# Product 4's second Strassen step in nine more groups, and the rotation in the next group's first four units

## The reference

```python
h = rmsnorm(x, norm_g[layer])
proj = h @ w_in[layer]                      # 1024 x 1024 @ 1024 x 12288
b_a, c_a, x_a, z_a, q, k, v, z_b, g_a, g_b = jnp.split(proj, split_points, axis=-1)
y_a = short_conv_branch(b_a, c_a, x_a, z_a, conv_w[layer], conv_b[layer], w_a_out[layer])
y_b = retention_branch(q, k, v, z_b, w_b_out[layer])   # q and k turned by rotary()
merged = jax.nn.sigmoid(g_a) * y_a + jax.nn.sigmoid(g_b) * y_b
x = x + merged @ w_o[layer]

def rotary(t, cos, sin):
    t1, t2 = jnp.split(t, 2, axis=-1)
    return jnp.concatenate([t1 * c - t2 * s, t1 * s + t2 * c], axis=-1)
```

## Time and profile before

| what | us |
|---|---|
| median of 3 runs | 1373.87 (1373.47 to 1374.01) |
| the profiled execution, its time | 1375.26 |
| its span in the profile | 1372.3 |
| TensorE busy | 1360.4 |
| VectorE, ScalarE, GpSimd busy | 1065.8, 584.5, 431.3 |
| groups 10 to 18 (from 539.84 to 882.58) | 342.7 |

### The profile page before, as it was taken

How to read it: one execution, slowest core, us unless ns; L and a number is a source line. 1 busy time by engine, 2 the same in 40 slices (tenths; PEclk the granted TensorE clock), 3 DMA queues, 4 the chain that set the end, 5 groups by cost and what they waited for, 6 DMA issues and landing times.

```text
span 1372.3 us, 16470 instructions
## 1 busy us (share of the span) xinstructions
PE 1360.4 (99%) x6336; PEld 1135.3 (83%) x6336; DVE 1065.8 (78%) x1008; ACT 584.5 (43%) x792; POOL 431.3 (31%) x313
## 2 busy tenths in 40 slices
PE   9999999999999999999999999999999999999997
PEld 7788888888888888888888888888888888888886
DVE  6898474578877777778888888648776998788887
ACT  6844233323222232233333333337778433443445
POOL 0100232244555554543443444315444000100002
PEclk9999999999999999999999999999999999999999
DMA  9746313322212222355544444557767699945443
GB/s 326 216 135 213 110 62 123 123 77 77 77 51 67 68 63 64 120 154 153 151 124 119 116 143 146 185 191 248 255 236 258 137 330 316 236 162 199 158 88 123
DMA packets 106125, 212.71 MB, mean 155 GB/s; under 512 B 6976, under 2 KB 49088, under 8 KB 101184
## 3 DMA queue, kind: packets, MB, share of 16 engines
q1 hardware_dynamic: 103024, 193.82, 42.5%
q0 software_dynamic: 2880, 17.83, 6.6%
q10 hardware_dynamic: 144, 0.02, 0.0%
HBM read 148.20 MB, written 55.05 MB: 148 GB/s over the span
## 4 chain that ended last, share of the span: by engine, by line
PE 91%; ACT 2%; DVE 2%; issue 2%; DMA 1%; POOL 1%; SPq 1%; POOLq 0%; ACTq 0%; DVEq 0%
PE psum L2488 17%; PE psum L2486 17%; PE psum L2489 17%; PE psum L2623 7%; PE psum L2625 7%; PE psum L2624 7%; PE psum L2413 3%; PE psum L2416 3%; PE psum L2415 3%; PE psum L2531 2%; PE psum L2533 2%; PE psum L2532 2%; PE psum L2430 1%; PE psum L2432 1%; PE psum L2431 1%
## 5 line engine op out<-in xcount | busy, mean ns | idle before, releaser
L2486 PE MATMUL psum<-hc,slots 128*128 128x512 f32 x1048 | 407.7, 389 | 0.0
L2488 PE MATMUL psum<-hc,slots 128*128 128x512 f32 x1048 | 407.7, 389 | 0.0
L2489 PE MATMUL psum<-hc,slots 128*128 128x512 f32 x1048 | 407.7, 389 | 0.0
L1087 ACT ACTIVATE slots<-work 128x1024 fp32r<-128x1024 f32 (+1 forms) x149 | 155.4, 1048 | 486.1 <-PE psum L2489 390.5
L1581 DVE TENSOR_TENSOR slots<-work,slots 128x1024 fp32r<-128x1024 f32 (+1 forms) x149 | 215.3, 1445 | 44.1 <-ACT slots L1087 44.1
L2489 PEld LDWEIGHTS psum<-hc,slots 128*128 128x128 f32 x1048 | 196.7, 188 | 40.9
L2486 PEld LDWEIGHTS psum<-hc,slots 128*128 128x128 f32 x1048 | 196.7, 188 | 40.5
L2488 PEld LDWEIGHTS psum<-hc,slots 128*128 128x128 f32 x1048 | 196.7, 188 | 40.5
L1347 ACT ACTIVATE last_slot<-arena 128x1024 fp32r<-128x1024 f32 x112 | 118.6, 1062 | 163.2 <-PE psum L2625 157.4
L2623 PE MATMUL psum<-last_slot 128*128 128x512 f32 (+1 forms) x452 | 175.3, 388 | 0.0
L2625 PE MATMUL psum<-last_slot 128*128 128x512 f32 (+1 forms) x452 | 175.0, 387 | 0.0
(11 more groups left out here) (214 smaller groups left out, 2092.3 us busy)
## 6 DMA issues: line engine op xcount, KB each, us to landing
work<-w_channel SPq DMA_DIRECT2D x80, 512.0 KB, 3.6
arena<-w_last SPq DMA_DIRECT2D x19, 1024.0 KB, 7.6
qk<-qk_scratch SPq DMA_DIRECT2D x32, 512.0 KB, 3.6
arena<-w_last POOLq DMA_DIRECT2D x9, 1024.0 KB, 10.6
v_raw<-value_scratch SPq DMA_DIRECT2D x32, 256.0 KB, 3.9
arena<-gate_scratch SPq DMA_DIRECT2D x16, 512.0 KB, 7.5
value_c<-w_value SPq DMA_DIRECT2D x10, 512.0 KB, 4.8
rows_of_x<-x_rows SPq DMA_DIRECT2D x8, 512.0 KB, 9.4
```

Source lines behind the costliest of these rows:

```text
L1087: nc.scalar.activation(slots[:, u % SLOTS, 0, 0:columns_of(u)], src, ACT.Copy).then_inc(w_hi, 1)
L2486: nc.tensor.matmul(bank, slot[:, 0, w], x_high, start=product in STARTS and j == 0, stop=False, skip_group_check=True)
L2488: nc.tensor.matmul(bank, slot[:, 0, w], x_low, start=False, stop=False, skip_group_check=True)
L2489: last = nc.tensor.matmul(bank, slot[:, 1, w], x_high, start=False, stop=j == 3, skip_group_check=True)
```

## The change

`TWICE` reaches to group 18 now, so the eight turning groups and the gate group behind them take the second step too. They get an eighth unit, the four quarter sums on GpSimd and the four adds on VectorE; the kept quarter is loaded again in group 19 and no longer in group 10. The rotation's first three steps leave p = 6 of their own group; all of it lies in the next group's units 0 to 3, the first half's parts (`turned(g, 0)`) at p = 2, those of the second half at p = 4 as before. On GpSimd the silu product of piece 0 moves ahead of S1, S3 and S2. On ScalarE `turned(g - 1, 0)` moves from p = 1 to p = 2, behind `silu(g - 1, 3)`.

```diff
--- before.py
+++ after.py
@@ -47,7 +47,7 @@
 GATES_B, CONVS, QZS = range(0, 2), range(2, 10), range(10, 18)
 
 
-TWICE = range(1, CONVS.stop)
+TWICE = range(1, GROUPS - 1)
 UNIT_TABLE = [(g, p) for g in range(GROUPS) for p in range(8 if g in TWICE else 7)]
 UNITS = VALUE_UNITS + len(UNIT_TABLE)
 
@@ -959,12 +959,13 @@
                 silu(g - 1, 3)
             if g in TWICE:
                 second_sums(g)
+            if turn:
+                silu(g, 0)
             if g + 1 < GROUPS:
                 s1(g + 1)
                 s3(g + 1)
                 s2(g + 1)
             if turn:
-                silu(g, 0)
                 silu(g, 1)
             if g + 1 < GROUPS:
                 s4(g + 1)
@@ -1473,8 +1474,9 @@
 
                         if g < GROUPS:
                             first(g)
+                        silu(g - 1, 3)
+                    if p == 2:
                         turned(g - 1, 0)
-                        silu(g - 1, 3)
                     if p == 4:
                         turned(g - 1, 1)
             if g >= GROUPS:
@@ -2029,11 +2031,12 @@
                         conv_tap(last, 2)
                         conv_y(last)
                 if kind_of(last) == "turn":
-                    for step in {0: (3, 4, 5)}.get(p, ()):
+
+                    for step in {0: (0,), 1: (1, 2, 3, 4, 5)}.get(p, ()):
                         turn(last, 0, step)
-                    if p == 1:
+                    if p == 2:
                         turned(last, 0)
-                    for step in {1: (0,), 2: (1, 2, 3), 3: (4, 5)}.get(p, ()):
+                    for step in {2: (0, 1), 3: (2, 3, 4, 5)}.get(p, ()):
                         turn(last, 1, step)
                     if p == 4:
                         turned(last, 1)
@@ -2044,9 +2047,6 @@
                     conv_early(g)
                 if p == 6:
                     conv_product(g, 1)
-            if kind_of(g) == "turn" and p == 6:
-                for step in range(3):
-                    turn(g, 0, step)
             if g == GROUPS - 1:
                 if p in (4, 5):
                     retention_begins(p - 4)
```

## The result

The changed kernel takes 1376.24 us in the median of 22 runs (1375.31 to 1378.38), the kernel before 1373.24 in 22 runs of its own: a ratio of 1.0022 with a 95% interval of 1.0015 to 1.0028, 3.0 us slower. The predicted 1376.2 stood on a median before of 1373.87, so the predicted difference was +2.3 and the measured one is +3.0; that 1376.2 and 1376.24 agree so closely is luck. The slowdown is clear of zero, but the interval reaches from 0.15% to 0.28%, so on which side of the prediction's bound of 0.2% it lies stays open.

What follows compares the result with a forecast made beforehand. TensorE, 99% busy, set the pace, but a 38.55 us VectorE-GpSimd-ScalarE loop would exceed its 37.60 us per group. Gain -4.3 plus waits 6.4 gave +2.1, taken as +2.3: 1373.87 + 2.3 = 1376.2 us, range 1371.2 to 1379.0.

Steps and rivals of the forecast that it cites:

- TensorE's gain of 0.48 per group: Second Strassen step in groups 10 to 18 shortens each from 38.08 to 37.60 us, 4.3 us (0.31%) for nine.
- VectorE and GpSimd one at a time: VectorE operations with two SBUF inputs and GpSimd sums or products exclude each other: 35.0 of 37.60 us after the change.
- rival 3: Only the 0.74 us quarter sums don't exclude VectorE: 37.87 us in eight groups, -2.2 in all, 1371.7 us; chance 0.07.
- The early hand-over: A GpSimd sum waiting behind a VectorE operation gets going 0.15 us before that ends, taking 2.85 instead of 2.40.
- rival 5: No early hand-over, every hold lasts to the recorded end: 39.3 us per group, +7.4, 1381.3 us; chance 0.06.
- The loop of 38.55 us: VectorE, GpSimd and ScalarE from product 6's low part to the next group's: 22.75 + 15.80 us, where TensorE needs 37.60.
- two pairs of rotation parts: Item of 1.22 us in VectorE's 19.26 us stretch from product 6's low part to product 4's first low part.
- the walk: Each engine's operations laid end to end in the new order: 38.55 us per group, +2.1 us in all.
- Where TensorE waits: Product 5, until product 6's sum leaves its banks: 0.55 us in group 12, 0.97 in groups 13 to 18, 6.4 total.
- rival 4: S3 precedes the next group's first low part, delaying the last quarter product: 0.65 us in eight groups, +0.9, 1374.8; chance 0.06.
- My shift from +2.1 to +2.3: Total difference raised because varying one constant at a time gave +1.2 to +4.8, half the cases under +2.4.
- Rival 2, the other side: Holds fall elsewhere, 4.4 instead of 5.37 us, and the loop fits: TensorE never waits, -4.3, 1369.6 us; chance 0.16.

## Why the prediction was right

- *TensorE's gain of 0.48 per group, 4.3 in all.* Right: groups 10 and 11 have 37.59 us, and the three versions in which TensorE hardly waits come to -3.8 to -4.1.
- *VectorE and GpSimd one at a time.* Right in each row that I looked up, for the short sums as well: the quarter sums took 1.12 and 1.18 us beside VectorE instead of 0.74, which ends rival 3 (its 37.87 us can't be had from the printed terms, which give 38.55 - 0.86 = 37.69; nothing hangs on it). The early hand-over holds for them: the rotation part that the first of them met ended at 678.99 and the sum at 679.59, 0.60 behind it, where it takes 0.74 alone. That ends rival 5.
- *The loop of 38.55 us.* Measured 38.61 to 38.64, and shown to be one by its members. Two GpSimd products shortened and another order of VectorE's work brought the group down to TensorE's length, and the place of a GpSimd product and a ScalarE operation brought it up to what was laid out before (40.6 and 39.7 us). No run changed the quarter sums, S1, S2 or S3 by themselves; their part rests on the rows. (The "two pairs of rotation parts" in the walk are one pair, the first half's: 1.22 us is two operations, and the trace has them at 669.86 and 670.46. The sum is right.)
- *Where TensorE waits.* Product 5, seven times, 0.95 us and 0.07 at the start behind it, where I had 0.97; no wait in front of the last quarter product, so not rival 4. Its mechanism, S3 in front of the low part, shows in two of the experiments: in the version with the second step alone, where the held rotation operations behind it make most of the wait, and in the one with two products short.
- *The term that was mis-sized is the first group with a wait.* I had 0.55 us for group 12 and 38.13 us of length; it has 1.06 and 38.65. In group 11 the eighth unit's high part started 0.37 us behind the last quarter sum, where group 13 shows 0.09; it set off the loop's full length a group earlier than the walk. Why it was late there is open, and no run tested whether it alone made the difference. The walk's nine groups are 2 x 37.58 + 38.13 + 6 x 38.55 = 344.59 us, the measured ones 345.58: of the 1.0 between them 0.52 is group 12 and 0.45 the 0.06 to 0.09 by which the loop is longer in the other six. My shift from +2.1 to +2.3 covered a part of this by luck: it came from the spread of the constants and not from group 12.
- *Rival 2, the other side,* is what a better order gives: a hold less, and the loop fits. The condition that I set for it, 4.4 us of holds or less, is met by the version with the rotation in units 2 and 3: 2.44 in its two low parts, 0.82 in the quarter sums, 1.0 in S3 and 0.04 in S2, about 4.3 us by its rows.

## What to carry to other kernels

A kernel whose TensorE is busy for 99% of the time can still be a microsecond per iteration away from another bound: follow the other engines round once, from one operation to the same operation of the next iteration, and compare that length with the iteration of the engine that sets the pace. Where two engines exclude each other, their order decides, not the sum of their work; put the long runs of the one where the other is idle or touches something else, and let it do the operations that aren't held (here the adds from PSUM) beside the other's sums. A wait in such a loop is paid again in every iteration, so half of an optimization can cost more (+49.5 us) than the whole of it can bring (-4.1).

## What the runs showed of the hardware

- With waits of 4.2 to 5.0 us (second step only) TensorE's granted clock fell to 0.50 around the end of the wait and stayed there for about 3 us; with the waits of 0.8 to 1.8 us in the other kernels the mean of a group stayed at 1.00.
- A GpSimd memset of 128x512 took 0.54 us and ran beside a VectorE operation with two SBUF inputs without either being held; the product of the same size took 1.30 and held VectorE for up to 1.10.
